# Issue positions of the dilated branch's bases and accumulating loads, and of four output-pair loads, in a one-core decoder layer

## The reference

```python
h = rms_norm(x, g_attn[l]);  proj = h @ w_in[l]          # q, k, v of both mixers, gates ga and gb
o_a = merge_heads(fox_attention(q_a, k_a, v_a, log_f))   # 8 heads of 128
o_b = merge_heads(dilated_attention(q_b, k_b, v_b, slopes))   # 8 heads of 128
merged = jax.nn.sigmoid(ga) * (o_a @ w_br_fox[l]) + jax.nn.sigmoid(gb) * (o_b @ w_br_dil[l])
x = x + merged @ w_out[l]
h = rms_norm(x, g_ffn[l]);  u = h @ w_up[l]
...                                                       # causal convolution over 3 rows, silu(gate) * val
x = x + (hidden) @ w_down[l]
```

## Time and profile before

| | us |
|---|---|
| median of 3 runs | 1332.25 |
| the three runs | 1339.04, 1332.13, 1332.25 |
| the profiled execution's own time | 1339.04 |
| its span in the profile | 1337.2 |
| TensorE busy in it | 1327.1 |
| VectorE, ScalarE, POOL busy | 1157.8, 966.0, 176.0 |

### The profile page before, as it was taken

The page is one execution under the profiler, slowest core; times in us unless marked ns, Lnnn a source line. Parts: engine busy times, 40 slices in busy tenths (PEclk is TensorE's granted clock), DMA queues, the critical chain, the costliest instruction groups (busy, mean ns, idle before and its releaser), DMA issues.

```text
span 1337.2 us, 16581 instructions
## 1 busy us (share of the span) xinstructions
PE 1327.1 (99%) x6031; PEld 1099.5 (82%) x6031; DVE 1157.8 (87%) x1387; ACT 966.0 (72%) x1226; POOL 176.0 (13%) x193
## 2 busy tenths in 40 slices
PE   9999999999999989999999999999999999999998
PEld 7888888888888878888888888888888888888887
DVE  6868787888888777888789898999999999999998
ACT  7666666666666655667778777888888888888874
POOL 0121212021011120000010102021111112020200
PEclk9999999999999989999999999999999999999999
DMA  9877685759888786678969788999999899999996
GB/s 360 290 170 251 142 266 119 246 142 244 242 207 225 253 227 193 203 217 275 280 173 334 156 308 173 315 209 292 235 271 257 235 276 224 296 211 314 193 291 178
DMA packets 123443, 317.29 MB, mean 237 GB/s; under 512 B 12249, under 2 KB 13537, under 8 KB 123105
## 3 DMA queue, kind: packets, MB, share of 16 engines
q1 hardware_dynamic: 93008, 236.67, 50.9%
q0 software_dynamic: 25728, 75.51, 31.7%
q10 hardware_dynamic: 4624, 4.05, 0.9%
HBM read 314.08 MB, written 2.11 MB: 236 GB/s over the span
## 4 chain that ended last, share of the span: by engine, by line
PE 95%; DMA 2%; DVE 1%; ACT 1%; issue 0%; POOL 0%; ACTq 0%; POOLq 0%
PE acc L939 11%; PE acc L943 11%; PE acc L941 11%; PE acc L977 9%; PE acc L981 9%; PE acc L979 9%; PE acc L1168 4%; PE acc L1164 4%; PE acc L1166 4%; PE acc L1141 3%; PE acc L1143 3%; PE acc L1139 3%; DMA raw<-w_fox 2%; PE acc L1378 1%; PE acc L958 1%; PE acc L962 1%
## 5 line engine op out<-in xcount | busy, mean ns | idle before, releaser
L2240 DVE TENSOR_TENSOR w_lo<-raw,w_hi 128x1024 fp32r<-128x1024 f32 x224 | 271.5, 1220 | 61.0 <-ACT w_hi L1596 60.1
L1596 ACT ACTIVATE w_hi<-raw 128x1024 fp32r<-128x1024 f32 x224 | 234.0, 1054 | 79.8 <-PE acc L943 26.3
L939 PE MATMUL acc<-w_hi,actA 128*128 128x512 f32 x580 | 228.3, 394 | 0.0
L943 PE MATMUL acc<-w_hi,actA 128*128 128x512 f32 x580 | 226.1, 390 | 0.0
L941 PE MATMUL acc<-w_lo,actA 128*128 128x512 f32 x580 | 225.8, 389 | 0.0
L1596 ACT ACTIVATE w_hi<-raw_y 128x1024 fp32r<-128x1024 f32 x154 | 160.5, 1058 | 78.5 <-PE acc L943 26.7
L2240 DVE TENSOR_TENSOR w_lo<-raw_y,w_hi 128x1024 fp32r<-128x1024 f32 x154 | 185.3, 1219 | 19.3 <-ACT w_hi L1596 17.9
L2240 DVE TENSOR_TENSOR w_lo<-raw_x,w_hi 128x1024 fp32r<-128x1024 f32 x118 | 142.2, 1220 | 47.7 <-ACT w_hi L1596 47.3
L1596 ACT ACTIVATE w_hi<-raw_x 128x1024 fp32r<-128x1024 f32 x118 | 121.8, 1052 | 49.5 <-DMA raw_x<-w_in 19.7
L943 PEld LDWEIGHTS acc<-w_hi,actA 128*128 128x128 f32 x580 | 108.9, 188 | 22.8
L939 PEld LDWEIGHTS acc<-w_hi,actA 128*128 128x128 f32 x580 | 108.9, 188 | 22.0 <-issue 0.2
(11 more groups left out here) (421 smaller groups left out, 2803.8 us busy)
## 6 DMA issues: line engine op xcount, KB each, us to landing
raw<-w_in SPq DMA_DIRECT2D x101, 512.0 KB, 4.7
raw<-w_down SPq DMA_DIRECT2D x59, 512.0 KB, 5.5
raw_x<-w_up SPq DMA_DIRECT2D x44, 512.0 KB, 4.9
raw_y<-w_up POOLq DMA_DIRECT2D x34, 512.0 KB, 7.8
raw_x<-w_in SPq DMA_DIRECT2D x28, 512.0 KB, 3.9
odd<-w_up SPq DMA_DIRECT2D x27, 512.0 KB, 5.0
work<-w_up SPq DMA_DIRECT2D x24, 512.0 KB, 5.4
work<-w_up POOLq DMA_DIRECT2D x24, 512.0 KB, 8.1
```

Source lines behind the costliest of these rows:

```text
L939: nc.tensor.matmul(o, lhsT=a_h, rhs=w_hi[:, s, k, :], start=first and k == 0, stop=False, skip_group_check=onto_seed)
L943: mm = nc.tensor.matmul(o, lhsT=a_l, rhs=w_hi[:, s, k, :], start=False, stop=last and k == KU - 1, skip_group_check=onto_seed)
L1596: nc.scalar.activation(w_hi[:, n % RING, :, :], src.rearrange("p (k n) -> p k n", k=KU), ACT.Copy).then_inc(hi_done, 1)
L2240: nc.vector.tensor_tensor(w_lo[:, n % RING, :, :], src.rearrange("p (k n) -> p k n", k=KU), w_hi[:, n % RING, :, :].bitcast(f32), ALU.subt ...
```

## The change

Two tables and the order of POOL's list change. The bases are issued after loads 4, 5, 6 and 7 (before: 5, 6, 8 and 9), and in another order of products. The four pair loads are issued after loads 22, 23, 24 and 26 (before: 26 to 29). POOL issues the adds in a new order, and its two waits for used fox units are gone.

```diff
-PAIR_LOADS_AT = {26: (1, 0), 27: (1, 1), 28: (0, 0), 29: (0, 1)}
-DIL_BASE_AT = {5: "P7", 6: "P6", 8: "P5", 9: "P4"}
+PAIR_LOADS_AT = {22: (1, 0), 23: (1, 1), 24: (0, 0), 26: (0, 1)}
+DIL_BASE_AT = {4: "P4", 5: "P6", 6: "P7", 7: "P5"}
...
+            add_dil_tile("P4", 1)
+            add_dil_tile("P6", 1)
+            prepare_dil(13).then_inc(prep_ready, 1)
             add_dil_tile("P7", 1)
-            prepare_dil(13).then_inc(prep_ready, 1)
-            add_dil_tile("P6", 1)
-            pool.wait_ge(used, BR_AT["F", 1, 1] + 1)
             add_dil_tile("P5", 1)
+            add_dil_tile("P4", 2)
             prepare_dil(14).then_inc(prep_ready, 1)
             add_dil_tile("P6", 2)
-            pool.wait_ge(used, BR_AT["F", 1, 3] + 1)
-            add_dil_tile("P4", 1)
+            add_dil_tile("P4", 3)
             prepare_dil(15).then_inc(prep_ready, 1)
-            add_dil_tile("P4", 2)
-            add_dil_tile("P4", 3)
             third_sum(PAIRS, 0)
```

## The result

| | before | changed |
|---|---|---|
| median, us | 1333.22 (6 runs) | 1341.12 (6 runs) |
| lowest to highest | 1331.79 to 1339.04 | 1340.17 to 1343.06 |
| profiled execution's own time | 1339.04 | 1344.05 |
| its span | 1337.2 | 1342.3 |

The ratio of the changed kernel's time to that of before is 1.0055, 95% interval 1.0034 to 1.0077: 7.9 us slower between the medians. In the runs beside the first experiments the kernel before stands at 1331.7 (27 runs), so about 1332 is its usual time, and the execution profiled for the earlier trace rows, 1339.04, was one of its rare long ones (6 of its 80 runs on record took 1336 us or more). That is why the profiled pair, 1339.04 and 1344.05, differs by 5.0 us only.

What follows compares the result with a forecast made beforehand. TensorE, busy 1327.1 of 1337.2 us, bounds the kernel; only its waits and clock can change. 1331.65 + 7.3 (wait) + 3.15 (clock) - 0.56 - 0.63 (other waits) = 1341 us; overall range 1331 to 1347.

Steps and rivals of the forecast that it cites:

- Step 1: SP's queue, branch stage: the fourth base now lies ahead of load 9, 1.34 us more to drain.
- Steps 2 and 3: POOL's queue: five adds instead of two; load 9 lands at 476.6, TensorE waits 7.3 us (2.3 to 12.8).
- the lag of 3 us: DMA engines: about 3 us of the slowest engine's 3.9 us lag put ahead of base P4's landing, at 457.7.
- The clock after the wait: TensorE after the long wait for head 12's copy: the fall of the clock paid again, 3.15 us.
- Step 4: TensorE near 516.68: P4's third add goes out earlier, gain 0.56 us (0 to 0.56).
- Step 5: Pair loads moved earlier: VectorE sum wait near 545 goes, gain 0.63 us or a loss of the same size.
- The path as I wrote it: Branch stage: DMA of load 9, ScalarE's high half 1.06 us, copy 0.47 us, then TensorE.
- my base of 1331.65 us: Profiled execution 1339.04 us less the long wait, 4.24 us, and its slow clock, 3.15 us.
- A: Rival, load 9: the lead hides the adds and bases, not slower, 1330.5 to 1334 us; chance 0.26.
- B: Rival, head 13's copy: a second long wait, slower still, 1347 to 1353 us; chance 0.10.
- C: Rival, branch stage: faster by over 0.5%, all waits and slow clock sum to 8.6 us; chance 0.04.

Runs made afterwards that it cites:

- e1: Changed kernel with the four pair loads back after loads 26 to 29, so moved bases and adds alone: 1339.83 us, ratio 1.0058.
- e3: Kernel before with only the four bases issued after loads 4, 5, 6 and 7 in the new order: 1331.98 us, ratio 1.0005.
- e4: e1 with all adds except P4's first held until TensorE has used F(1,0): 1334.67 us, ratio 1.0021.
- e11: e1 with the seven adds issued as plain copies on POOL's queue, weight tile sums not formed: 1334.51 us, ratio 1.0015.
- e2: Kernel before with only the four pair loads issued after loads 22, 23, 24 and 26: 1333.38 us, ratio 1.0009.
- e7: e1 with ScalarE's copy of the transposed probabilities two high halves earlier: 1341.11 us, ratio 1.0068.
- e6: Changed kernel with ScalarE's copy of the transposed probabilities two high halves earlier: 1344.02 us, ratio 1.0090.
- e8: Kernel before with only POOL's two waits for used units taken out: 1335.19 us, ratio 1.0025.

## Why the prediction was right

*Time and sign.* 1341 forecast, 1341.12 measured. The named mechanism, adds ahead of load 9 that make head 12's copy late, is the one that e1, e3, e4 and e11 confirm. That the number fits to 0.1 us is luck, as told below.

*Step 1, bases.* Costed at one more plain transfer, 1.34 us. e3 shows 0.2 us, not distinguishable from nothing, but with P7's add 3.5 us later than before. In that combination the early bases cost nothing; their 1.34 us is not shown.

*Steps 2 and 3, adds and load 9.* Issues forecast at 458, 461, 466, 474, 475, measured 456.6, 460.5, 466.1, 471.0, 471.8; landing of load 9 forecast 476.6, measured 476.2 (461.1 + 15.0); wait 7.3 against 6.69. The price of an add held (2.85 us forecast, 2.84 in the changed kernel), and so did the turn-taking of the queues (268 against 277 packets from 462 to 466). The range of waits, 2.3 to 12.8, covers e1's 8.08. Inside the timeline two terms were off and made up for each other: base P4 landed at 456.4, 1.3 us behind load 4 (455.1), where I had put 1.34 and a lag of 3 us; base P5 landed at 470.7, not 473.9, and from there to load 9 it took 5.4 us, not 2.7. So the run does not show the lag of 3 us where I put it. And "the engines were full" is not enough for the 13.5 us that load 9 took in the profile of before: in e2 they were full as well (busy share 1.08 or more from 464 to 472, by the windows), with the same two adds, and it took 9.5. I built the timeline on an execution that was not typical.

*The clock after the wait* was mis-sized: 3.15 us "paid again", 1.6 measured, 2.0 in e1. The lower level had been granted 3.6 us before TensorE went on, in e1 2.8 us, in the profile of before 0.7 us; the part of the low clock that fell on the idle TensorE cost nothing.

*Step 4.* The wait near 516 is gone, as forecast, but that does not show the gain: it is gone in e2 and e3 too, where the adds keep their old order. By these traces it belonged to the long execution.

*Step 5, the pair loads: the sign was wrong.* I put a gain of 0.63 us with a loss of the same size as its bound. The 0.63 us wait did go (it is missing in e1 and e3 too, with the pair loads in their old places), but an earlier sum became late: 1.98 us of waiting and 1.7 us of half clock in the profiled execution, 1.6 us in the median by e2. I had checked the lead of the weights, which was ample, and not what else is queued behind their halves on VectorE.

*The path as I wrote it was too narrow.* "Load 9, high half, copy, TensorE" is what the trace shows, but e7 shows another one beside it, "load 10, high half, low half, head 13's softmax, TensorE", with 6.10 us; moving the copy freed nothing.

*Why the sum came out.* Own time of the profiled execution, less TensorE's waits from the branch stage on and less the slow clock on work, is nearly the same everywhere: before 1339.04 - 5.43 - 3.0 = 1330.6, e1 1340.46 - 8.08 - 2.0 = 1330.4, e2 1333.38 - 3.01 = 1330.4, e3 1332.01 - 1.25 = 1330.8, changed 1344.05 - 10.07 - 3.3 = 1330.7. So the waits and the clock are the whole difference. Against the kernel's usual 1331.7 us, e1 measures the long wait with its clock at 8.1 us, where my terms gave 7.3 + 3.15 - 0.56 = 9.9; the pair loads were taken at -0.6 and are +1.6. The two errors, -1.8 and +2.2, cancel. Of the -1.8, 1.25 is the short wait for line 1608 that the usual executions have (e2, e3) and my base of 1331.65 us had not. That base fits the median of 27 later runs, 1331.7, because it kept 0.56 + 0.63 us of other waits in its place, which e2 and e3 do not have: luck too. The wait of 1.40 us near 594 in the changed kernel's profile stands behind a high half that waited 3.23 us for the DMA into raw_x; it has no counterpart in e1 or e2, nor in e6, which has both parts of the change; it is open.

*The rivals.* A (hidden by the lead) is refuted for the adds; the early bases alone are hidden (e3). B's second long wait, at head 13's copy, did not come in the changed kernel. C needed the long wait as a rule in the runs of before, and 6 of 80 are that long. The Trainium skill, "DMA: Bandwidth & Descriptors", section Rules for kernel authors, says to issue a DMA early and wait on it late. That cost nothing measurable for the bases (e3, ratio 1.0005) and 8.1 us with the adds (e1).

## What to carry to other kernels

Background transfers that nobody waits for still have a place in time: if their queue takes turns with the one that feeds the critical engine, spread them, and count an accumulating transfer by the engine time that it occupies, here twice a plain one. A wait that seems to slow an engine down (POOL's two waits for used units) can be what paces such traffic. And when a load is late, ask not only who reads it but what stands behind its reader in every in-order queue; here moving one victim ahead exposed the next. Last, before a timeline is built on one profiled execution, compare its own time with the other runs: this one was 7 us longer than most.

## What the runs showed of the hardware

An accumulating DMA of 0.524 MB occupied the 16 engines for 2.84 us (changed kernel, packets of 1.9 KB), a plain one on the same queue for 1.38 (e11, packets of 3.7 KB). With both queues at work they passed 268 and 277 packets in 4 us. Load 9 took from 9.5 us (e2) to 13.5 us (before) from issue to landing behind the same three bases and with the same two adds on the way.

The granted clock fell while TensorE stood idle, and the loss in slow work did not grow with the wait: 3.0 us for 4.24 us of waiting (before), 1.6 for 6.69 (changed), 2.0 for 8.08 (e1). Waits of 1.25 (e3), 1.79 (e2) and 2.85 us (e8) were followed by no such fall, while one of 1.98 us, 60 us after a first fall, was.
